# Byte offsets of the SBUF tiles in a two-layer hybrid trunk: small tables first, stationary tiles at multiples of 128

## What is computed

```python
for i in range(DEPTH):                                    # DEPTH = 2
    h = rms_norm(x, norm_mix[i])
    mem_kv = rms_norm(mem, norm_mem[i]) @ w_mem_kv[i]     # 256 x 2048 @ 2048 x 1024
    if i % 2 == 0:
        q_a, k_a, v_a, q_m = _split(h @ w_in_a[j], A_SPLITS)     # ... @ 2048 x 2432
        mix = swa_sink_attention(...)
    else:
        q_b, f_b, i_b, g_b, q_m = _split(h @ w_in_b[j], B_SPLITS) # ... @ 2048 x 6656
        mix = hgrn2_chunkwise(...) ...
    mem_out = memory_attention(q_m, mem_k, mem_v)
    x = x + jnp.concatenate([mix, mem_out], axis=-1) @ w_o[i]    # ... @ 2048 x 2048
    gate, up = _split(rms_norm(x, norm_ffn[i]) @ w_gate_up[i], (D_FF, D_FF))  # ... @ 2048 x 11264
    x = x + (jax.nn.silu(gate) * up) @ w_down[i]                 # 256 x 5632 @ 5632 x 2048
```

## Time and profile before

| | us |
|---|---|
| median of 3 runs (2292.48 to 2293.86) | 2292.94 |
| the profiled execution | 2292.81 |
| its span | 2291.1 |
| PE busy, matmuls | 2272.7 (99%) |
| PEld busy, weight loads | 1880.4 (82%) |
| DVE busy | 1271.0 (55%) |
| ACT busy | 1007.5 (44%) |
| POOL busy | 55.9 (2%) |
| mean granted clock of TensorE | 1.00 of full speed |

### The profile page before, as it was taken

One profiled execution on the slowest core, in us unless ns is written; L12 is line 12 of the kernel. 1 busy time (PEld: TensorE's weight loads), 2 busy tenths in 40 slices (PEclk: granted clock), 3 DMA queues, 4 the chain that ended last, 5 costly groups with the idle time before them and its releaser, 6 DMA issues.

```text
span 2291.1 us, 29587 instructions
## 1 busy us (share of the span) xinstructions
PE 2272.7 (99%) x10710; PEld 1880.4 (82%) x10710; DVE 1271.0 (55%) x1498; ACT 1007.5 (44%) x1242; POOL 55.9 (2%) x85
## 2 busy tenths in 40 slices
PE   8999999999999999999999999999999999999999
PEld 6888888888888888888888888888888888888887
DVE  6756665555555554444556666665555555554443
ACT  5656544444444443344443434344444444443332
POOL 2101000000000000000000000000000000000000
PEclk9999999999999999999999999999999999999999
DMA  7564446666666665655554545456666666666664
GB/s 247 171 201 128 131 156 195 189 189 189 190 186 190 192 184 178 193 185 185 175 145 144 164 147 165 147 184 184 192 187 189 189 187 192 185 191 195 199 193 130
DMA packets 213277, 410.29 MB, mean 179 GB/s; under 512 B 13264, under 2 KB 13516, under 8 KB 213196
## 3 DMA queue, kind: packets, MB, share of 16 engines
q1 hardware_dynamic: 212108, 407.11, 58.8%
q10 hardware_dynamic: 1088, 2.10, 0.2%
HBM read 407.06 MB, written 2.10 MB: 179 GB/s over the span
## 4 chain that ended last, share of the span: by engine, by line
PE 92%; DVE 1%; issue 0%; ACT 0%; POOL 0%; DVEq 0%; ACTq 0%
PE unit_bank L1364 86%; PE mix_bank L1385 2%; PE mix_bank L1520 2%; PE mix_bank L1451 0%; PE mix_bank L1414 0%; DVE w_lo L833 0%; PE mix_bank L1423 0%; PE mix_bank L1505 0%; DVE tanh_q L1065 0%; PE mix_bank L1460 0%; PE mix_bank L1435 0%; PE mix_bank L1549 0%; PE mix_bank L1547 0%; PE mix_bank L1540 0%; PE mix_bank L1530 0%
## 5 line engine op out<-in xcount | busy, mean ns | idle before, releaser
L833 DVE TENSOR_TENSOR w_lo<-raw,w_hi 128x1024 fp32r<-128x1024 f32 x768 | 936.9, 1225 | 826.9 <-ACT w_hi L488 817.2
L488 ACT ACTIVATE w_hi<-raw 128x1024 fp32r<-128x1024 f32 x768 | 810.5, 1060 | 973.0 <-PE unit_bank L1364 947.7
L1364 PE MATMUL unit_bank<-w_hi,hT_hi 128*128 128x512 f32 (+1 forms) x1984 | 778.0, 392 | 0.0
L1364 PE MATMUL unit_bank<-w_hi,hT_lo 128*128 128x512 f32 (+1 forms) x1984 | 771.2, 389 | 0.0
L1364 PE MATMUL unit_bank<-w_lo,hT_hi 128*128 128x512 f32 (+1 forms) x1984 | 770.2, 388 | 0.0
L1364 PEld LDWEIGHTS unit_bank<-w_hi,hT_lo 128*128 128x128 f32 x1984 | 372.4, 188 | 77.1
L1364 PEld LDWEIGHTS unit_bank<-w_lo,hT_hi 128*128 128x128 f32 x1984 | 372.7, 188 | 74.0
L1364 PEld LDWEIGHTS unit_bank<-w_hi,hT_hi 128*128 128x128 f32 x1984 | 372.6, 188 | 74.1 <-issue 0.3
L1364 PE MATMUL unit_bank<-w_hi,gT_hi 128*128 128x512 f32 x704 | 279.5, 397 | 0.0
L1364 PE MATMUL unit_bank<-w_hi,gT_lo 128*128 128x512 f32 x704 | 279.1, 396 | 0.0
L1364 PE MATMUL unit_bank<-w_lo,gT_hi 128*128 128x512 f32 x704 | 279.0, 396 | 0.0
(11 more groups left out here) (227 smaller groups left out, 1114.7 us busy)
## 6 DMA issues: line engine op xcount, KB each, us to landing
raw<-in_w_gate_up SPq DMA_DIRECT2D x352, 512.0 KB, 4.2
raw<-in_w_down SPq DMA_DIRECT2D x176, 512.0 KB, 4.5
raw<-in_w_in_b SPq DMA_DIRECT2D x104, 512.0 KB, 4.3
raw<-in_w_o SPq DMA_DIRECT2D x64, 512.0 KB, 4.0
raw<-in_w_in_a SPq DMA_DIRECT2D x40, 512.0 KB, 3.9
raw<-in_w_mem_kv SPq DMA_DIRECT2D x32, 512.0 KB, 4.5
mem_tok<-in_mem SPq DMA_DIRECT2D x4, 512.0 KB, 8.8
x_tok<-in_x SPq DMA_DIRECT2D x4, 512.0 KB, 8.5
```

The lines of the kernel that those rows point to most:

```text
L488: act.activation(w_hi[:, s, :, :], raw[:, s, :, :], ACT.Copy).then_inc(sems["hi_ready"], 1)
L833: dve.tensor_tensor(w_lo[:, s, :, :], raw[:, s, :, :], w_hi[:, s, :, :].bitcast(F32), ALU.subtract).then_inc(sems["lo_ready"], 1)
L1364: ins = pe.matmul(unit_bank[2 * pair + tile][:, 0:cols], a, b[:, s, j, 0:cols], start=opens and n == 0 and j == 0 and m == 0, stop=closes ...
```

## The change

Tables and small columns, 12 of them, are placed ahead of `x_tok`; `keep` takes a `line` to which an offset is rounded up, 32 as before but for `x_tok`, where it is 2048. So `x_tok`, `hT`, the rings and what follows move up by 1920 bytes, from a rest of 128 after division by 2048 to a multiple of 2048. The arena starts at a multiple of 128 in place of 32, which moves it and all in it up by 32 bytes, from 138976 to 139008. (The other edited line writes `2 * half + 3 * half` as `5 * half`, which is the same.) No instruction is added, taken away or moved on any engine; only addresses differ.

```diff
-        def keep(name, shape, dtype=F32):
+        def keep(name, shape, dtype=F32, line=32):
             size = int(np.prod(shape)) * 4
-            place[0] = -(-place[0] // 32) * 32
+            place[0] = -(-place[0] // line) * line
             t = at(name, shape, dtype, place[0])
             place[0] += size
             return t
 
-        x_tok = keep("x_tok", [TILES, D])
+        ident = keep("ident", [P])
+        q_gain = keep("q_gain", [HD_A])
+        k_gain = keep("k_gain", [HD_A])
+        g_gain = keep("g_gain", [HD_B])
+        cos = keep("cos", [TILES, ROT])
+        sin = keep("sin", [TILES, ROT])
+        ang = keep("ang", [TILES, ROT])
+        turn = keep("turn", [TILES, ROT])
+        freq = keep("freq", [ROT])
+        pos_int = keep("pos_int", [TILES], I32)
+        sum_sq = keep("sum_sq", [TILES, BLOCKS])
+        sum_two = keep("sum_two", [TILES, 2])
+        x_tok = keep("x_tok", [TILES, D], line=2048)
         hT = (keep("hT_hi", [KT, SEQ], F32R), keep("hT_lo", [KT, SEQ], F32R))
         raw = keep("raw", [RING, 2, COLS])
...
-        arena = -(-place[0] // 32) * 32
+        arena = -(-place[0] // 128) * 128
```

More of the change, by code:

```diff
@@ L172, in trunk @@
         squares = keep("squares", [COLS])
-        ident = keep("ident", [P])
         level_mask = keep("level_mask", [LEVELS, P // 2])
         columns = keep("columns", [ROWS])
-        q_gain = keep("q_gain", [HD_A])
-        k_gain = keep("k_gain", [HD_A])
-        g_gain = keep("g_gain", [HD_B])
         sink = keep("sink", [KV_A * GROUP_A])
         minus_sink = keep("minus_sink", [KV_A * GROUP_A])
[L181 to L186, removed]
         lb_work = keep("lb_work", [4, HEADS_B])
@@ L189, in trunk @@
         decay_now = keep("decay_now", [3, 4])
-        sum_sq = keep("sum_sq", [TILES, BLOCKS])
-        sum_two = keep("sum_two", [TILES, 2])
         mem_sum_sq = keep("mem_sum_sq", [TILES, BLOCKS])
@@ L236, in trunk @@
         mixT = (take("mixT_hi", [KT, SEQ], F32R), take("mixT_lo", [KT, SEQ], F32R))
-        take = arena_map(2 * half, 2 * half + 3 * half)
+        take = arena_map(2 * half, 5 * half)
         q_a = take("q_a", [TILES, COLS])
```

## The result

The changed kernel takes 2270.8 us (median of 4 runs, 2270.30 to 2271.51) against 2292.8: a ratio of 0.990, 95% interval 0.989 to 0.992. That is 22.0 us less; I had said 24.2, and 2268.7 us. The profiled execution has a span of 2268.8 us against 2291.1, 22.3 us less.

A forecast was written before the change was run, and what follows sets the result against it. TensorE's matmul pace was taken as the bound. 2292.8 (profiled execution) - 24.8 for `gT`, `mixT` and `memT` + 0.6 kept back = 2268.6, given as 2268.7 us against the median; range 2263 to 2283.

The forecast's parts named there:

- The bound: Whole kernel: time is the sum of TensorE's matmul costs; weights, splits and transfers are early almost everywhere.
- The sum: L1364 with arena tiles: `gT` 16.1 us, `mixT` 5.8, `memT` 2.9, together 24.8 us saved, less 0.6 us kept back.
- That term: `mixT` and `memT` stages: 0.6 us of the saving lost to ACT and DVE chains and weight waits; bounds nothing to 8.7.
- The cause: L1364: a stationary block beginning inside a line costs one more line's read, 7.6 ns a matmul; rest 0 removes it.
- The term for the rings: Rings and `hT` moving to multiples of 2048: taken as 0; either way at most 45 us on 5952 matmuls.
- rival 4: `gT`: pace goes by something finer, such as distance to the moving operand; half the gain, 2280.8 us; 5 in 100.
- Rivals 1 to 3: Region, 2292.9 us, 8 in 100; `hT` and rings lose, 2314, 3 in 100; `hT` gains too, 2223.5, 4 in 100.
- Region: `gT`, `mixT`, `memT`: slow because they lie far up or by side of the rings; no change, 2292.9 us; 8 in 100.
- `hT` loses or gains by starting at 2048: `hT` matmuls at L1364: slower, 2314 us, 3 in 100; or faster with all others, 2223.5 us, 4 in 100.
- The feeders: Transfers and splits for `gT` pieces: keep up at 2.72 us a piece in place of 2.81, so no new wait.
- The rule of the pages: Warm matmul takes N / 2.4 + 2.5 ns, 216 ns for 512 columns, no address term; change worth nothing, 2292.9 us.
- The small matmuls: L1505 and L1520, float32: 275 ns against 272 of transposes; address gain taken as nothing, 1.8 us kept for lower end.

The follow-up runs named there:

- the runs with 2289.2 and 2271.4 us: The kernel before with only the arena's line changed: arena at 139008 took 2289.2 us, arena at 139136 took 2271.4 us.
- three rests: Changed kernel with stationary tiles at other rests after division by 128: `gT` 64, `mixT` 16 (high) and 48 (low), `memT` 32; 2290.5 us.
- `w_lo` off: Changed kernel with `w_lo` and `gT_lo` both moved up by 32 bytes, all else in place; 2313.0 us.

## Why the prediction was right, and where it wasn't

**The bound** was right. TensorE's pace set the time in all the runs, and the price of an edit was matmuls times nanoseconds, with the paces as each trace shows them: 14.1 us worked out against 14.0 measured for `gT_lo`, 5952 x 6.6 = 39 against 35.9 for `hT`, 5952 x 6.6 + 3264 x 7.6 = 64 against 58.0 for the rings. Where the measured number is the smaller one, the attention and recurrence stages hid most of the rest: in the run with `hT` off they took 8.4 us more where the price would give some 11. The working left one thing out that changes nothing: PE's waits of before are 13.8 us in all, not the 7.0 that it names; 5.1 of them are for a DMA at the start. ACT's wait for PE fell from 947.7 to 930.8 us, 17 us where "some 20 us" were forecast.

**The sum** was right in its largest term: `gT` 2112 x 7.6 = 16.1 us, and 16.0 came. `mixT` gave 4.4 in place of 5.8 and `memT` 1.3 in place of 2.9. I had put 0.6 us for what these two stages keep back; it is 3.0, of which 1.7 are waits. That term was mis-sized, inside the bounds that it had (nothing to 8.7), and with the 0.6 us of the `hT` stages it makes the 2 us between 24.2 and 22.0.

**The cause** was wrong, and that the number came out right all the same was luck. What held was only that the three tiles fall to `hT`'s pace, and they did so because the new offsets happen to leave a distance of 0. The step that failed reads: "I take it that a stationary block that begins inside a line costs the read of one more line". The run with everything off by 32 has each block begin inside a line of 64 or 128 bytes, at no cost (226.7 ns); the arena at a multiple of 128 alone has none that do, and is slow (233.0 ns in the mean). What counted in their place was the distance to the ring, 0 or not after division by 256. What I had seen in the trace, "the slower one goes with exactly the three tiles whose offset leaves 96 after division by 128", was true of a second property as well: their distance to the ring leaves 160 after division by 256, that of `hT` leaves 0. One kernel with two groups of tiles can't tell such properties apart.

**The term for the rings** failed with it. I took 0 for their move by 1920 bytes, since `kmT_a` and `kmT_b` show that "a moving operand's rest is worth nothing". The rings' move turned a gain of 4 us into one of 22. I gave the right cause 5 in 100 and only as a way to get half: rival 4 has "the distance to the moving operand" in it. That the arena ends on the right line of 256 after the change is worth noting: 139008 is a multiple of 256 by the sizes of the tables, where the code asks for 128 only, and the rings follow from the 2048.

**Rivals 1 to 3** are out. Region: `hT` off by 32 is slow in place. `hT` loses or gains by starting at 2048: 226.7 before and after. The feeders kept up in the faster down stage, with PE busy in 243.00 of 243 us:

```profile
842.00:1085.00 243.00, 243.00 (x1090) 201.64 (x1089) 121.36 (x111) 101.30 (x108) 0.00 (x0) 1.00 0.61 191
```

**The rule of the pages** that stood against the change, no term for an address in the pace of a matmul (the Trainium skill, TensorE: Matmul & The Clock Gate, "Back-to-back issue gap"), would have had the time stay; the runs with 2289.2 and 2271.4 us differ by nothing but 128 bytes in the arena's place, so the measurement decides. The other one, that an operand need only start at a multiple of its element size (the Trainium skill, SBUF — State Buffer, "Operand start alignment"), is about legality; for the time the run with all off by 32 shows that here a rest by itself costs nothing. The prediction also took the two paces as speaking against loads that cost the running matmul nothing; the runs show a relation between addresses, and no run shows what the load and the stream do to each other.

**The small matmuls** (L1505, L1520) kept their 275 ns with `key` moved from rest 96 to 0, so the 3 ns weren't the rest, as I had taken. Both their operands lie in the arena and moved together, so they say nothing on the distance.

## What to carry to other kernels

If matmuls of the same shape run at two paces in one trace, list the offsets of both operands, not of one, and look at their difference before settling on alignment. In this kernel the 512-column matmuls of L1364 are fastest if the stationary tiles and the moving rings all leave the same rest after division by 256; the rest itself is free (0, 32 and 128 were tried). And where two tiles differ in the suspected property, undo each half of a layout change alone: halves that don't add up say that a relation is at work.

## What the runs showed of the hardware

- For these matmuls (128 x 128 stationary, 512 columns moving, fp32r) each distance tried between stationary tile and ring that isn't a multiple of 256 bytes costs 6 to 8 ns in the mean on top of 226.7 (5 to 6 where only `w_lo` and `gT_lo` were off). It shows in the starts and in the modelled durations (medians of mostly 392 to 400 in place of 389 ns), and hardly in the loads' records, whose medians stay at 187 or 188 ns but for two groups of `mixT` (192 with three rests, 189 with `w_lo` off).
- One misplaced tile out of two spoils the whole group of three matmuls (700 ns in place of 680), not its own steps alone. How the load and the stream get in each other's way, and why the group's total is nearly the same at all wrong distances, is open.
- With 384 columns (`hT` alone) the pace is 173.3 ns at distance 0, 176.6 in the mean at 96, and 173.3 at 32. So at that width one wrong distance costs and another doesn't; no run explains it.
- Float32 matmuls with 256 columns and transposes with 128 show no price at distances of 128 and 160 (1.89 us for eight scores and 109 ns a transpose, as at 0).
- Only multiples of 32 and one pair of multiples of 16 (240 and 208) were tried as distances, and only in this kernel's order of three matmuls per pair of blocks.
